# Moving the third layer's neighbourhood attention in between the pieces of its projection, and issuing dense pieces by kind of product

## The reference, cut to what matters

```python
x = x + 0.5 * rmsnorm_2(swiglu_2(rmsnorm_2(x, ffn1_pre_g), ...), ffn1_post_g)
h = rmsnorm_2(x, mix_pre_g[l])
qkv = (h @ w_qkv[l]).reshape(B, S, 3, N_HEADS, HEAD_DIM).transpose(2, 0, 3, 1, 4)   # 1024 x 3072
o_na  = neighbourhood_attention(q[:, :8], k[:, :8], v[:, :8], na_rel_bias)   # 8 heads
o_dil = dilated_mixture_attention(q[:, 8:], k[:, 8:], v[:, 8:], t5_bias)     # 8 heads
o_na, o_dil = rmsnorm_2(o_na, na_out_g), rmsnorm_2(o_dil, dil_out_g)         # each over 512 columns
mixed = jnp.concatenate([o_na, o_dil], axis=-1) @ w_out[l]                   # 1024 x 1024
x = x + rmsnorm_2(mixed, mix_post_g[l])
x = x + 0.5 * rmsnorm_2(swiglu_2(rmsnorm_2(x, ffn2_pre_g), ...), ffn2_post_g)
```

## Time and profile before

| | us |
|---|---|
| median of 3 runs (2142.53 to 2153.58) | 2143.8 |
| the profiled execution's own time | 2144.65 |
| its span, first to last instruction | 2142.6 |
| PE busy | 2048.6 (96%) |
| DVE busy | 1662.6 (78%) |
| ACT busy | 1345.5 (63%) |
| granted PE clock, mean | 0.972 |

### The profile page before, as it was taken

How to read it: one execution, slowest core, us unless ns; L and a number is a source line. 1 busy time by engine, 2 the same in 40 slices (tenths; PEclk the granted TensorE clock), 3 DMA queues, 4 the chain that set the end, 5 groups by cost and what they waited for, 6 DMA issues and landing times.

```text
span 2142.6 us, 26414 instructions
## 1 busy us (share of the span) xinstructions
PE 2048.6 (96%) x9581; PEld 1682.3 (79%) x9586; DVE 1662.6 (78%) x2034; ACT 1345.5 (63%) x1869; POOL 57.9 (3%) x92
## 2 busy tenths in 40 slices
PE   8978999997999999999999999999999999889998
PEld 7757788885778888888888888888877887777887
DVE  5777777776679999999999999999986555356555
ACT  4354444445358878888888878888864445465443
POOL 0000000010000000000000000000000000000000
PEclk8989999998799999999999999999999999989999
DMA  9913588580269999999999999999975554304551
GB/s 396 390 53 133 227 319 318 206 329 31 80 264 380 375 373 360 368 371 363 375 361 374 367 369 373 360 370 366 369 270 210 190 187 154 137 21 178 195 177 59
DMA packets 81944, 578.40 MB, mean 270 GB/s; under 512 B 9264, under 2 KB 9904, under 8 KB 13600
## 3 DMA queue, kind: packets, MB, share of 16 engines
q1 hardware_dynamic: 71264, 516.98, 63.1%
q0 software_dynamic: 8112, 53.38, 6.5%
q10 hardware_dynamic: 2448, 6.42, 0.9%
HBM read 574.65 MB, written 2.10 MB: 269 GB/s over the span
## 4 chain that ended last, share of the span: by engine, by line
PE 88%; DVE 6%; ACT 3%; DMA 2%; issue 1%; POOL 0%; ACTq 0%; DVEq 0%; POOLq 0%
PE ps L618 26%; PE ps L620 26%; PE ps L619 26%; DMA Z<-in_ada 1%; PE ps L860 1%; PE ps L889 1%; PE ps L1043 1%; PE ps L874 1%; DVE weights_low L1892 1%; ACT arena L1466 1%; PE ps L720 1%; PE ps L789 1%; PE ps L564 1%; PE ps L655 1%; DVE ps L2119 0%
## 5 line engine op out<-in xcount | busy, mean ns | idle before, releaser
L2421 DVE TENSOR_TENSOR weights_low<-ring,weights_high 128x1024 fp32r<-128x1024 f32 x668 | 794.9, 1222 | 45.6 <-ACT weights_high L1576 36.7
L1576 ACT ACTIVATE weights_high<-ring 128x1024 fp32r<-128x1024 f32 x668 | 705.0, 1060 | 91.1 <-PE ps L620 77.6
L618 PE MATMUL ps<-weights_high,xt_high 128*128 128x512 f32 x1832 | 737.0, 402 | 13.6 <-DVE weights_low L1892 5.4
L620 PE MATMUL ps<-weights_high,xt_low 128*128 128x512 f32 x1832 | 720.0, 393 | 0.0
L619 PE MATMUL ps<-weights_low,xt_high 128*128 128x512 f32 x1832 | 719.4, 393 | 0.0
L1245 ACT ACTIVATE weights_high<-ring 128x1024 fp32r<-128x1024 f32 x298 | 314.0, 1059 | 295.7 <-PE ps L620 289.8
L1892 DVE TENSOR_TENSOR weights_low<-ring,weights_high 128x1024 fp32r<-128x1024 f32 x298 | 361.9, 1223 | 157.1 <-ACT weights_high L1245 155.2
L618 PEld LDWEIGHTS ps<-weights_high,xt_high 128*128 128x128 f32 x1832 | 347.5, 190 | 84.9 <-DVE weights_low L1892 6.1
L620 PEld LDWEIGHTS ps<-weights_high,xt_low 128*128 128x128 f32 x1832 | 347.0, 189 | 74.4
L619 PEld LDWEIGHTS ps<-weights_low,xt_high 128*128 128x128 f32 x1832 | 348.0, 190 | 68.2 <-issue 0.8
L618 PE MATMUL ps<-weights_high,hT_high 128*128 128x512 f32 x688 | 268.6, 390 | 1.2 <-DVE hT_low L2431 1.2
(11 more groups left out here) (270 smaller groups left out, 1408.5 us busy)
## 6 DMA issues: line engine op xcount, KB each, us to landing
ring<-in_stream SPq DMA_DIRECT2D x483, 1024.0 KB, 5.9
Z<-in_ada POOLq DMA_DIRECT2D x40, 1024.0 KB, 5.6
Z<-in_ada SPq DMA_DIRECT2D x4, 1024.0 KB, 11.4
ring<-in_ada SPq DMA_DIRECT2D x2, 1024.0 KB, 18.3
arena<-in_ada SPq DMA_DIRECT2D x2, 1024.0 KB, 25.7
Z<-in_na POOLq DMA_DIRECT2D x1, 2048.0 KB, 10.5
Z<-in_dil POOLq DMA_DIRECT2D x1, 2048.0 KB, 17.0
band<-in_band ACTq DMA_DIRECT2D x2, 768.0 KB, 16.0
```

The source lines that it names most:

```text
L618: nc.tensor.matmul(out, xh, wh, start=n, stop=False, skip_group_check=True)
L620: return nc.tensor.matmul(out, xl, wh, start=False, stop=last, skip_group_check=True)
L1576: act.activation(WH[:, slot, :], raw, ACT.Copy).then_inc(m["hi_ready"], 1)
L2421: nc.vector.tensor_tensor(WL[:, slot, :], raw, WH[:, slot, :].bitcast(F32), ALU.subtract).then_inc(m["lo_ready"], 1)
```

## The change

1. **Weight layout.** The host reorders the projection's columns to N q, N k, N v, L q, L k, L v (one group each), and the output projection's four chunks.
2. **Order on PE.** `projection(4, 7)` is replaced by `wide_projection(7)`: dense pieces as before, and between them all eight fills, the whole of units N00 to N11 and the score of L00. `wide_attention` keeps the other L work. PROJ, the fills and the units' buffers get other places (`wide_words`, `wide_den`, FS, Z; fills in banks 0 to 3; turned probabilities in banks 6, 7; values in banks 0, 2, 4, 5).
3. **Order on ACT and DVE.** Their splits and copies for the projection are interleaved with the N units' bias, probabilities, copies and stores in one written order.
4. **Output projection.** It starts with the k tiles of the N half for both column groups, then turns the L half, then does the L k tiles.
5. **Dense pieces by kind.** `up_piece` issues its twelve matmuls in three runs of four: high by high after `hi_ready` (and `xt_hi`), high by low after `lo_ready`, low by high after `xt_ready`. Pieces that report a first row block (the last one of each output projection) keep the old order.

```diff
             def up_piece(chunk, half, banks, pair, t=None, first_rows=None):
+                slot = piece_no(chunk, half) % SPLITS
+                if first_rows is not None:
...
+                if t is not None:
+                    pe.wait_ge(xt_hi, 4 * SPLIT_NO[t] + pair + 1)
+                pe.wait_ge(hi_ready, piece_no(chunk, half) + 1)
+                products(XTH, WH, True, False)
+                pe.wait_ge(lo_ready, piece_no(chunk, half) + 1)
+                products(XTH, WL, False, False)
                 if t is not None:
                     pe.wait_ge(xt_ready, 4 * t + pair + 1)
...
+                products(XTL, WH, False, True).then_inc(piece_done, 1)
...
+            def wide_projection(t):          # PE
...
+                for q in range(2):
+                    for pair in range(4):
+                        up(q, pair)
+                for pair, name in enumerate(("N00", "N10", "N01", "N11")):
+                    up(2, pair)
+                    wide_fill(name)
+                up(3, 0)
+                score(LAYERS, "N00")
+                up(3, 1)
+                score(LAYERS, "N10")
+                up(3, 2)
+                up(3, 3)
+                up(4, 0)
+                pe.wait_ge(gemm_out, gemm_outs(2 * LAYERS) + 8)
+                turn(LAYERS, "N00")
+                up(4, 1)
+                values(LAYERS, "N00")
+                wide_fill("L00")
+                up(4, 2)
+                turn(LAYERS, "N10")
+                score(LAYERS, "N01")
+                wide_fill("L10")
+                up(4, 3)
+                values(LAYERS, "N10")
+                score(LAYERS, "N11")
+                up(5, 0)
+                turn(LAYERS, "N01")
+                wide_fill("L01")
+                up(5, 1)
+                values(LAYERS, "N01")
+                up(5, 2)
+                turn(LAYERS, "N11")
+                score(LAYERS, "L00")
+                wide_fill("L11")
+                up(5, 3)
+                values(LAYERS, "N11")
+
             def wide_attention():            # PE
...
+                score(LAYERS, "L10")
+                turn(LAYERS, "L00")
+                score(LAYERS, "L01")
+                values(LAYERS, "L00")
+                turn(LAYERS, "L10")
+                score(LAYERS, "L11")
+                values(LAYERS, "L10")
+                turn(LAYERS, "L01")
+                turn_wide(0)
+                turn_wide(1)
+                values(LAYERS, "L01")
+                turn(LAYERS, "L11")
+                values(LAYERS, "L11")
...
+            def wide_projection(t):          # ACT, from group 4 on
...
+                hi(4, 1)
+                probabilities(LAYERS, "N00")
+                hi(4, 2)
+                hi(4, 3)
+                copy_out(3)
+                probabilities(LAYERS, "N10")
+                hi(5, 0)
+                copy_pT(LAYERS, "N00")
...
+            def wide_projection():           # DVE, from group 4 on
...
+                lo(4, 0)
+                bias(LAYERS, "N00")
+                lo(4, 1)
+                bias(LAYERS, "N10")
+                lo(4, 2)
+                lo(4, 3)
+                lo(5, 0)
+                lo(5, 1)
+                store(LAYERS, "N00")
+                lo(5, 2)
+                bias(LAYERS, "N01")
+                lo(5, 3)
+                store(LAYERS, "N10")
+                bias(LAYERS, "N11")
...
+    qkv = i["w_qkv_2"][0].reshape(D, 3, 2, 512).transpose(0, 2, 1, 3).reshape(D, 3 * D)
```

More of the change, by code:

```diff
@@ L2321, in wide_attention @@
+                bias(LAYERS, "L01")
+                store(LAYERS, "L00")
+                asked = ask_wide_root(0)
+                bias(LAYERS, "L11")
+                wide_root(asked, 0)
+                store(LAYERS, "L10")
+                ahead_lo(GEMM_CHUNK[5], (3,))
+                store(LAYERS, "L01")
                 xt_split_lo(8, 0)
-                dve.wait_ge(pT_ps, TURNED(LAYERS, names[7]))
-                ahead_lo(GEMM_CHUNK[5], (1,))
+                store(LAYERS, "L11")
                 xt_split_lo(8, 1)
-                wide_root(1)
```

308 lines of the change are left out of this document (194 added, 114 removed).

## The result

The changed kernel took 2119.05 us (median of 4 runs, 2114.6 to 2124.23), and the kernel before, run beside it, 2145.89 (4 runs, 2142.53 to 2153.58). The ratio is 0.987, with a 95% interval of 0.985 to 0.989: 1.3% faster. The forecast was 2124.5, with 2119 to 2134 as the range of 8 in 10: the median lies on its lower edge, and the ratio, put on the 2143.8 on record before, gives 2115.9. Its direction, and its sum for the stretch that is rebuilt, came out; the gain of the edit by kind was put at 3.2 us with bounds of 0 and 5, and is about twice that upper bound (10.3 us, measured alone).

A forecast was written before the change was run, and what follows sets the result against it. PE was taken to bound the kernel (88% of the chain), idling in the third layer's latency-bound attention. Gains of 16.1 + 3.2 = 19.3 from 2144.65 give 2125.3; less 0.85 for the median, 2124.5, range 2119 to 2134.

The forecast's parts named there:

- The stretch: Third layer's projection to output projection, first to last dense matmul: 149.9 us becomes 132.8, a gain of 17.1 at full clock.
- score N11: PE's wait ahead of unit N11's score, directly behind N10's value product and a scaling: 1.25 us of idle.
- score L10: PE's wait ahead of unit L10's score, directly behind N11's value product and a scaling: 0.7 us of idle.
- turn L10: PE's wait ahead of L10's turn, for bias and probabilities, in the L part that stays bare: 0.6 us.
- last value products: PE's wait ahead of the stretch's last value product, directly behind its turn and the turn's copy: 1.2 us.
- The clock: Even chance of one fall at 2 us, near L11's value products: 1.0 off the rebuilt stretch's gain, leaving 16.1.
- rival 1: The clock falls in the interleave too; three or four low stretches cost 7 to 9 us: about 2132. Chance 0.13.
- rival 2: The hand-written order stalls: ACT or DVE waits with splits behind it, 10 us lost: about 2135. Chance 0.13.
- Rival 3: Slower: changing the stationary tile with every matmul costs time in 2700 dense-piece matmuls: 2163. Chance 0.04.
- Dense pieces by kind, elsewhere: Outside the rebuilt stretch, pieces start before their low halves at stage starts and late weights: 3.2 us, bounds 0 and 5.
- Nothing else: No other gain: DMAs move the same chunks, and the host's reordering is outside the time.
- rival 5: More than summed: no clock fall, late scores hidden, the fall at 1610 gone: 2118 to 2120. Chance 0.07.

The follow-up runs named there:

- the second profile of the change: The changed kernel, no edit, measured and profiled once more: 2121.39 us, ratio 0.9888 to the kernel before.
- the old output order: The changed kernel with the output projection's first column group computed completely before the second, as before the change: 2120.71 us, ratio 0.9883.
- the interleave alone: The changed kernel with the old `up_piece`, so the old matmul order in every dense piece: 2131.84 us, ratio 0.9932.
- the filler in it: The changed kernel with eight unread matmuls ahead of the score of D00 in both early layers' attentions: 2122.26 us, ratio 0.987.

## Why the prediction was right and wrong, by its own steps

**The stretch: right.** Forecast 132.8 us, measured 132.14 and 133.23 from start to start, 132.4 and 133.5 with the slot of the last matmul. Idle: 4.2 forecast, 3.5 in the four waits over 0.15 (1.27 + 0.63 + 0.47 + 1.11). One by one: score N11 1.25 and 1.27, score L10 0.7 and 0.63, turn L10 0.6 and 0.47, last value products 1.2 and 1.11; the smaller ones, and the 0.15 ahead of the output projection, did not show. On the side of before, the trace has 13.7 us of idle and so 7.6 of low clock, where the prediction put 17.5 and 3.8; only their sum of 21.3 enters the forecast. The first profile before has long falls and the first one after has none: other pairs of profiles give 14.3 and more in place of 17.6. The splits never made PE wait, as the walk through ACT's and DVE's queues said.

**The clock: right in kind.** The forecast was an even chance of one fall at 2 us, behind the wait ahead of the last value products of L11. It falls there and nowhere else in the stretch: in the second profile of the change and in that of the old output order, and in none of the other five profiles that keep the wait. Its price was put at 2 us and is about 1.7. What lies behind the stretch takes 198.7 us in both profiles with the fall and 198.7 to 201.3 in the five without, so that the fall is not shown to cost the whole kernel anything. Between the units and the pieces the clock is 1.00 in all of them. The rule of the Trainium skill, "TensorE: Matmul & The Clock Gate", section "A second HAM failure mode: psum-queue depth-cycling", says that brief pauses of PE between groups of matmuls can make the clock go back and forth; the trace does not agree for this mix, in which a piece of 2.7 us stands between small groups. By the 1.00, rival 1 did not happen, and rival 2 has no wait in the profile.

**The stationary tile that changes with each matmul: costs nothing.** Rival 3 (slower, 2163) needed 7 ns per matmul. Twelve matmuls of the changed kernel, 1907.95 to 1910.67 above, take 2.72 us, which is 0.227 each, as in the earlier trace rows.

**The term that was mis-sized: "Dense pieces by kind, elsewhere", 3.2 with bounds 0 and 5.** Measured 10.3 alone (6.4 to 14.0), and 9.4 on top of the interleave (24.0 - 14.6). It has two parts.

- *Direct.* At the stage starts 0.7 at 225.80 and 0.7 at 421.58, as forecast. In the first feed-forward part 0.4 more (188.95 to 188.56), unforeseen. In the feed-forward part after the experts about 1, forecast 0.9: from its first turns to the next ones 192.7 to 194.1 us in five profiles without early starts, 191.6 to 193.7 in seven with them, so the size is uncertain. At 87.69, forecast 0.9, nothing that stands out: the wait ahead of the low half is 1.20 where it was 1.25, since four matmuls sooner only means that PE is at the next wait sooner. And some 1 us in the third layer's stretch, unforeseen: the 0.95 for `xt_low` at 1916.83 of the interleave alone. Together some 4: within the bounds.
- *Indirect.* About 4.2 us in the second layer's attention, by a fall of PE's clock that stays away. This term was put at nothing: neither the kinds' sum nor "Nothing else" has it. The prediction asked what happens to a wait that goes, and followed each until PE was full again. It did not ask what a shift of 1 or 2 us does to an attention 60 us further on that no edit touches. The trace of before had the answer's half: 0.50 for seventeen microseconds in a stretch where PE waits on a chain, a place where 4 us could come or go. That they went was luck: the delay on the changed kernel shows that a shift of the same size also brings them.

The pairs that carry this, second layer's attention in us: without early starts 79.28, 79.79, 79.79 and 79.76; with them 75.13, 75.92, 75.28, 75.26 and 75.27 (and 76.72 with the filler in it); delayed by 1.6 without them 75.02; delayed by 1.25 with them 80.00; with them and one other edit behind this stage 79.94. All but the last go by the arrival, and all thirteen by the moment of the first fall. The amount of late work in the stage is equal in all of them.

**The sum.** The times say 26.8 between the two medians and the traces 26.2, where 19.3 was forecast. Of the traces' 26.2 the stretch is 17.6 (17.1 forecast, less 1.0); the attention of the second layer 4.2 (nothing); the places of the kinds before it 2.4 (2.3, but that they agree is chance: 0.6 of it lies ahead of the first layer's attention, whose first fill comes anywhere from 109.8 to 110.9 us in the profiles without early starts and 109.1 to 110.8 with them, so that no gain is shown there); the feed-forward part after the experts and what stands ahead of the projection 2.1 (0.9). The rest is under 0.3 each. The 2119 also lies where rival 5 stood (2118 to 2120), and not by its route: the fall at 1610 is gone in this profile and there is none in the stretch, but the two late scores are not hidden, and the 4.2 of the attention is no part of it.

**Open.** Why the clock falls at these moments and not at others: the runs show that the arrival moves the first fall against the stage's own work, and that the length of the attention goes by that moment, not by what rule: the early starts bring the stage sooner and the copies bring it later, and from 3.0 to 3.7 us both lead to about 2. Early starts don't decide in every execution, and how often they fail was not counted: a profile is one execution, and the times alone do not say where its clock fell. The first layer's attention takes 74.2 to 79.5 us in kernels with and without early starts (74.93 and 79.20 in the kernel before itself). There too the moment of the first fall says something: the four profiles that have it 2.0 to 2.6 us behind the first fill take 74.8 to 75.2 us, the three that have it 3.5 to 3.9 us behind take 77.7 to 79.5, and those before and behind these moments 74.2 to 77.1. Nothing that was tried steers it. And the times give the kinds 9 to 10 us where the terms above add up to some 8: within the intervals, and not explained further.

## What to carry to other kernels

Put a latency-bound chain between dense pieces that have slack on the helper engines: each unit then costs only its work on PE, and here a walk of the queues forecast the four largest waits that were left to within 0.15 us each. Where a product needs several operands, begin with those that come first, above all at the start of a stage. And where a profile has long stretches at the low clock in a part that is not edited, put their cost into the range in both directions: anything ahead of them that shifts by a microsecond can take them away or bring them.

## What the runs showed of the hardware

- The time of 75 to 80 us of attention depends on when it starts, by where the first low clock falls behind its first fill: 1.9 to 2.2 us behind it in seven profiles with 75.0 to 76.7 us, 3.0 to 3.9 in five with 79.3 to 79.9, 0.2 in one with 80.0. In the kernel before, 1.6 us of useless copies ahead of it took 4.3 to 4.8 us out of it and 3 us out of the whole (ratio 0.9986, 0.9974 to 0.9998); in the kernel after, 1.25 us of them cost 8 us by the times (0.9927 against 0.9888), 5 to 6 of them in the trace.
- Executions of one kernel on one core range over 10 us (2142.4 to 2152.16 in 21 runs), and single stretches over 4 to 5 us (74.93 and 79.20 in two profiles of one kernel), with a different share of low clock in each.
- Filler matmuls behind an idle time run at the low clock themselves (nine of 128 x 512 in 4.05 us behind 3.3 us of idle) and delay what follows. Fillers that follow dense work without a pause kept the clock: 1.00 over the 6.8 us in which the kernel without them has 0.50, worth 1.9 us.
- For fp32 matmuls of 128 x 128 by 128 x 512 a new stationary tile with every matmul is as fast as one that stays for two: 0.227 us in both kernels.
